# Gate and up products made transposed, with high and low tokens side by side in one 512-column product

## The reference

```
def swiglu_ffn(x, w_gu, w_down):
    a, u = jnp.split(x @ w_gu, 2, axis=-1)
    return (jax.nn.silu(a) * u) @ w_down

x = layer_norm(DEEPNORM_ALPHA * x + 0.5 * swiglu_ffn(x, ffn1_w_gu[l], ffn1_w_down[l]), ...)
```

## Time and profile before

| | |
|---|---|
| median of 3 runs | 1339.62 us (1339.14 to 1340.37) |
| span of the profiled execution | 1336.4 us |
| TensorE busy | 1316.4 us (99%) |
| VectorE busy | 1017.8 us (76%) |
| ScalarE busy | 677.8 us (51%) |
| mean DMA rate | 199 GB/s |
| chain that ended last | TensorE 85%, VectorE 7%, ScalarE 3%, DMA 2% |

### The profile page before, as it was taken

How to read it: one execution, slowest core, us unless ns; L and a number is a source line. 1 busy time by engine, 2 the same in 40 slices (tenths; PEclk the granted TensorE clock), 3 DMA queues, 4 the chain that set the end, 5 groups by cost and what they waited for, 6 DMA issues and landing times.

```text
span 1336.4 us, 18974 instructions
## 1 busy us (share of the span) xinstructions
PE 1316.4 (99%) x7172; PEld 1117.9 (84%) x7172; DVE 1017.8 (76%) x1597; ACT 677.8 (51%) x1069; POOL 105.0 (8%) x153
## 2 busy tenths in 40 slices
PE   9999999999999999999999999999999999999997
PEld 7888888788888888888887888888889998799985
DVE  6676778887777677777688887677776789966897
ACT  6444445644544445444437534444446668357582
POOL 1011000011011001111010010111000000000000
PEclk9999999999999999999999999999999999999999
DMA  8976756438766657676656449677556563465530
GB/s 270 321 237 227 228 181 213 129 102 262 239 233 226 199 189 243 228 235 218 210 171 207 126 137 322 236 249 235 173 192 175 157 206 127 142 194 163 183 127 32
DMA packets 199210, 265.46 MB, mean 199 GB/s; under 512 B 21392, under 2 KB 144400, under 8 KB 198608
## 3 DMA queue, kind: packets, MB, share of 16 engines
q1 hardware_dynamic: 187408, 223.65, 51.7%
q0 software_dynamic: 11712, 40.60, 8.9%
HBM read 263.13 MB, written 1.07 MB: 198 GB/s over the span
## 4 chain that ended last, share of the span: by engine, by line
PE 85%; DVE 7%; ACT 3%; DMA 2%; issue 1%; SPq 0%; DVEq 0%; ACTq 0%
PE ps L814 26%; PE ps L815 26%; PE ps L816 26%; PE ps L898 4%; DVE w_lo L1306 2%; DMA w_raw<-in_ffn_w_gu 1%; ACT w_hi L1134 1%; PE ps L1042 1%; PE ps L1103 1%; ACT att L1242 1%; DMA w_raw<-in_w_in 1%; DVE arena L1597 1%; DVE few_first L1335 1%; PE ps L1077 1%; DVE y L1334 1%
## 5 line engine op out<-in xcount | busy, mean ns | idle before, releaser
L1306 DVE TENSOR_TENSOR w_lo<-w_raw,w_hi 128x1024 fp32r<-128x1024 f32 (+3 forms) x424 | 499.1, 1206 | 143.4 <-ACT w_hi L1134 140.2
L1134 ACT ACTIVATE w_hi<-w_raw 128x1024 fp32r<-128x1024 f32 (+3 forms) x424 | 433.2, 1046 | 243.3 <-DMA w_raw<-in_ffn_w_gu 129.4
L814 PE MATMUL ps<-w_hi,col_hi 128*128 128x512 f32 (+2 forms) x1024 | 396.4, 387 | 3.6 <-DVE w_lo L1306 2.2
L816 PE MATMUL ps<-w_hi,col_lo 128*128 128x512 f32 (+2 forms) x1024 | 391.4, 382 | 0.0
L815 PE MATMUL ps<-w_lo,col_hi 128*128 128x512 f32 (+2 forms) x1024 | 391.2, 382 | 0.0
L814 PEld LDWEIGHTS ps<-w_hi,col_hi 128*128 128x128 f32 x1024 | 192.7, 188 | 42.7 <-DVE w_lo L1306 4.0
L816 PEld LDWEIGHTS ps<-w_hi,col_lo 128*128 128x128 f32 x1024 | 192.4, 188 | 37.2
L815 PEld LDWEIGHTS ps<-w_lo,col_hi 128*128 128x128 f32 x1024 | 192.8, 188 | 33.8
L814 PE MATMUL ps<-w_hi,lat_hi 128*128 128x512 f32 (+2 forms) x544 | 208.9, 384 | 0.0
L816 PE MATMUL ps<-w_hi,lat_lo 128*128 128x512 f32 (+2 forms) x544 | 206.6, 380 | 0.0
L815 PE MATMUL ps<-w_lo,lat_hi 128*128 128x512 f32 (+2 forms) x544 | 206.3, 379 | 0.0
(11 more groups left out here) (148 smaller groups left out, 1180.1 us busy)
## 6 DMA issues: line engine op xcount, KB each, us to landing
w_raw<-in_ffn_w_gu SPq DMA_DIRECT2D x352, 256.0 KB, 4.4
w_raw<-in_w_in SPq DMA_DIRECT2D x108, 512.0 KB, 4.6
w_raw<-in_ffn_w_down SPq DMA_DIRECT2D x88, 512.0 KB, 4.7
mod<-in_w_ada POOLq DMA_DIRECT2D x32, 768.0 KB, 7.3
w_raw<-in_w_out SPq DMA_DIRECT2D x24, 512.0 KB, 4.5
norm_g<-in_ln_g POOLq DMA_DIRECT2D x8, 512.0 KB, 4.1
norm_b<-in_ln_b POOLq DMA_DIRECT2D x8, 512.0 KB, 5.7
w_raw<-in_w_out SPq DMA_DIRECT2D x16, 256.0 KB, 4.4
```

The costliest lines, as they stand in the source:

```text
L814: pe.matmul(dst, a_hi, b_hi, start=start, stop=False)
L816: return pe.matmul(dst, a_lo, b_hi, start=False, stop=stop)
L1134: act.activation(half_of(w_hi[j], n, h), half_of(raw[j], n, h), ACT.Copy).then_inc(hi_ready, 1)
L1306: tt(half_of(w_lo[j], n, h), half_of(raw[j], n, h), half_of(w_hi[j], n, h).bitcast(F32), ALU.subtract)\
```

## The change

From round 2 on (`BY_ROWS = 2`) the gate and up products are made transposed. Job `gt(r, m, part)` makes 128 hidden columns (`m` = 0 or 1) of the gate (`part` 0) or of up (`part` 1) for all 256 tokens. The stationary operand is now a 128-column tile of the weights, the moving operand the transposed tokens. High and low tokens lie side by side in one tile `col`, so that one product of 512 columns gives high weight x (high tokens, low tokens) in one bank, and one of 256 columns adds low weight x high tokens to its left half. Sixteen such products, eight of each kind, make one group, and four groups make a round. Each group has a bank of its own among 4, 5 and 6 in turn (`gt_bank`).

VectorE adds the two halves of the bank by one TENSOR_REDUCE over pairs, the gate's into `silu_rows`, the up's into `hidden`. ScalarE takes silu in place in SBUF, and VectorE multiplies. The result already has hidden columns on the partitions, so the transposes of rounds 2 to 10 are gone. Job `hcol` (per `m`) makes high and low parts straight from SBUF. Rounds 0 and 1 stay as they were, with `ht` for both. The `ht` of round 1 now comes after the first group of round 2.

A weight unit of gate and up is used in all four groups of a round, half the group for each unit. Unit (r,1) is first needed after 8 products, and unit (r,0) is given back after seven eighths of the round's gate and up work, where it was three quarters.

```
 ROUNDS = F // FU
 TAIL = 4
+BY_ROWS = 2
...
     for r in range(2, ROUNDS):
-        jobs += gu(r, 0) + [("ht", s, r - 1)]
+        jobs += gt(r, 0, 0) + [("ht", s, r - 1) if r - 1 < BY_ROWS else ("hcol", s, r - 1, 1)] + gt(r, 0, 1)
         if r > 2:
             jobs += [("spread", s, r - 3), ("modrow", s, r - 3)]
         if r < 2 + MOD_STEPS:
             jobs += [("modsum", s, r - 2)]
-        jobs += gu(r, 1)
+        jobs += gt(r, 1, 0) + [("hcol", s, r, 0)] + gt(r, 1, 1)
...
-    jobs += down(tail[0], 0) + down(tail[1], 0) + [("ht", s, ROUNDS - 1)] + down(tail[2], 0) + down(tail[3], 0)
+    jobs += down(tail[0], 0) + down(tail[1], 0) + [("hcol", s, ROUNDS - 1, 1)] + down(tail[2], 0) + down(tail[3], 0)
...
+def gt_bank(r, m, part):
+    return 4 + (4 * (r - BY_ROWS) + 2 * m + part) % 3
...
-        col_hi, _ = sb("col_hi", [P, KT, S], F32R)
-        col_lo, _ = sb("col_lo", [P, KT, S], F32R)
+        col, _ = sb("col", [P, KT, 2, S], F32R)
+        col_hi, col_lo = col[:, :, 0, :], col[:, :, 1, :]
...
+                elif kind == "gt":
+                    r, m, part, h = job[2:]
+                    if h == 0:
+                        bank_ready((s, r, m, part))
+                        if (r, gt_bank(r, m, part)) == (BY_ROWS, 6):
+                            turns_done(("ht", s, BY_ROWS - 1))
+                    for i in range(TT):
+                        tile_ready(s, i, h)
+                    hi, lo = parts_of(n)
+                    cols = slice(part * FU + m * P, part * FU + (m + 1) * P)
+                    b = gt_bank(r, m, part)
+                    for k in range(4):
+                        if k == 2:
+                            unit_ready(n, j, 1)
+                        kk = 4 * h + k
+                        if kk < KT - 1:
+                            pe.matmul(bank(b), hi[:, k, cols], col[:, kk, :, :].rearrange("p a s -> p (a s)"), start=kk == 0, stop=False)
+                        last = pe.matmul(bank(b, S), lo[:, k, cols], col_hi[:, kk, :], start=False, stop=False)
+                        if kk == KT - 1:
+                            last = pe.matmul(bank(b), hi[:, k, cols], col[:, kk, :, :].rearrange("p a s -> p (a s)"), start=False, stop=True)
+                    signal_end(last, n, j, (s, r, m, part) if h == 1 else None)
...
                 elif kind == "down":
                     r, i = job[2:]
-                    turns_done(("ht", s, r))
+                    if r < BY_ROWS:
+                        turns_done(("ht", s, r))
+                    else:
+                        pe.wait_ge(h_cols, at["h_cols", (s, r, 1)])
...
+                elif kind == "gt":
+                    r, m, part, h = job[2:]
+                    nth = at["silu", job[1:4]]
+                    if (part, h) == (1, 0):
+                        act.wait_ge(summed, at["summed", (s, r, m, 0)])
+                        act.activation(silu_rows[:, nth % 2, :], silu_rows[:, nth % 2, :], ACT.Silu).then_inc(silu_done, 1)
+                elif kind == "hcol":
+                    r, m = job[2:]
+                    act.wait_ge(hidden_done, at["hidden", (s, r, m)])
+                    act.activation(lat_hi[:, 2 * (r % 4) + m, :], hidden[:, r % 2, m, :], ACT.Copy).then_inc(hi_part, 1)
...
+                elif kind == "gt" and job[5] == 1:
+                    r, m, part, _ = job[2:]
+                    nth = at["hidden", job[1:4]]
+                    rows = silu_rows[:, nth % 2, :] if part == 0 else hidden[:, r % 2, m, :]
+                    name, value = ENDS[job[1:5]]
+                    dve.wait_ge(ends[name], value)
...
+                    dve.tensor_reduce(rows, bank(gt_bank(r, m, part)).rearrange("p (a s) -> p s a", a=2), AX_X, ALU.add).then_inc(summed, 1)
+                    if part == 1:
+                        dve.wait_ge(summed, at["summed", job[1:5]])
+                        dve.wait_ge(silu_done, nth)
+                        stt(rows, silu_rows[:, nth % 2, :], 0.5, rows, ALU.mult, ALU.mult).then_inc(hidden_done, 1)
+                elif kind == "hcol":
+                    r, m = job[2:]
+                    dve.wait_ge(hi_part, at["hi_part", job])
+                    q = 2 * (r % 4) + m
+                    tt(lat_lo[:, q, :], hidden[:, r % 2, m, :], lat_hi[:, q, :].bitcast(F32), ALU.subtract).then_inc(h_cols, 1)
```

More of the change, by code:

```diff
@@ L167, in ffn_jobs @@
     down = lambda r, i: [("down", s, r, i)]
+    gt = lambda r, m, part: [("gt", s, r, m, part, h) for h in range(2)]
     if s == 0:
@@ L282, in unit_of @@
         return s, ("gu", job[2], job[4])
+    if kind == "gt":
+        return s, ("gu", job[2], job[5])
     if kind == "down":
@@ L306, in columns_of @@
     ks, width, _ = unit_shape(*unit_of(job))
+    if kind == "gt":
+        return ks * width // 2
     if kind == "row":
@@ L421, in count_jobs @@
             turns[b] += 1
-        if kind in ("gu", "row", "T") and s != stage:
+        if kind in ("gu", "gt", "row", "T") and s != stage:
             held, step, readers, stage, buffers = {}, None, {}, s, []
@@ L426, in count_jobs @@
             n = NUMBER[got]
[L427 to L432, removed]
+            if kind == "gt":
+                first_half, last_half = (job[5] == h for h in range(2))
+                tile, group = None, job[1:5]
+            else:
+                last_half = kind in ("T", "down", "out") or job[4] == (1 if kind == "gu" else len(BLOCKS[KIND[s]][job[2]][0]) - 1)
+                first_half = kind in ("T", "down", "out") or job[4] == 0
+                tile = None if kind == "T" else job[3]
+                group = (s, job[2], tile) if kind in ("gu", "row") else (s, got[1], tile)
+            if kind in ("gu", "gt", "row", "T"):
+                bank = {"gu": lambda: gu_bank(s, job[2], tile), "gt": lambda: gt_bank(*job[2:5]),
                         "row": lambda: BLOCKS[KIND[s]][job[2]][3][tile], "T": lambda: TURNED[got[1]][0]}[kind]()
@@ L440, in count_jobs @@
                         held[bank] = ("hidden", COUNT.value["hidden", group])
+                    elif kind == "gt":
+                        COUNT.add("summed", group)
+                        COUNT.add(("silu", "hidden")[job[4]], job[1:4])
+                        held[bank] = ("summed", COUNT.value["summed", group])
                     elif not (kind == "row" and job[2] == "KV" and tile == 0):
@@ L455, in count_jobs @@
                     ENDS["sums", s, tile] = ENDS[group]
-        if kind in ("xt", "ht", "trlat", "ycols"):
+        if kind in ("xt", "ht", "hcol", "trlat", "ycols"):
             COUNT.add("hi_part", job)
+        if kind == "hcol":
+            COUNT.add("h_cols", job[1:])
         if kind == "ycols" and not TURN[job]:
@@ L838, in bank_ready @@
                     name, value = BANK_BEFORE[group]
-                    pe.wait_ge({"hidden": hidden_done, "copied": copied}[name], value)
+                    pe.wait_ge({"hidden": hidden_done, "summed": summed, "copied": copied}[name], value)
             def signal_end(last, n, j, group):
```

9 lines of the change are left out of this document (7 added, 2 removed).

## The result

| | before | after |
|---|---|---|
| median of 4 runs, us | 1339.99 (1339.14 to 1341.33) | 1352.67 (1351.30 to 1356.43) |
| span of the profiled execution, us | 1336.4 | 1349.2 |
| TensorE busy, us | 1316.4 | 1316.7 |
| VectorE busy, us | 1017.8 | 1106.7 |

The ratio is 1.0099, 95% interval 1.0086 to 1.0112. The change costs 1.0%. The forecast was 1341.4 in a range of 1334 to 1350, so the time lies above the range.

What follows compares the result with a forecast made beforehand. TensorE, busy 99% of the span, was taken as the bound. Its own -4.9 us plus stalls of 0.5, 2.9, 1.1, 0.4, 1.1 and 0.7 gave +1.8: span 1338.2, median 3.2 above it, so 1341.4 us, range 1334 to 1350.

Steps and rivals of the forecast that it cites:

- Ordinary rounds lose little: First sum done just in time for the fourth group in ordinary rounds; 0.5 us lost for all of them.
- T: The start of a round on TensorE; the fourth group was reckoned to start 8.6 us after it.
- Lateness shrinking: VectorE's round from first sum to next takes 15.4 us, under TensorE's 16.88, so lateness shrinks 1.5 us a round.
- TensorE's own work: Rounds from round 2 on: transposes give back 0.35 us, products add 0.21; 16.88 instead of 17.02, -4.9 us in all.
- The sum's price: Each VectorE sum of a bank's halves takes 0.686 us; VectorE's net added work is 2.9 us a round.
- The rival of a strided sum at 1.22 us: Reading PSUM with a step slows each sum, making VectorE the bound: about 1361 us; chance 0.10.
- the one of a pair at 0.36: Rival: a 512 and a 256 column product on TensorE together cost 0.36 us: about 1356 us; chance 0.05.
- The first bank in ordinary rounds: Fourth group wants the first group's bank 8.6 us into the round; its sum is done at 7.1 to 8.5.
- The rival with a stall in every round: Slipping loads make 28 modulated rounds wait at the first bank, 0.3 to 0.5 us each: about 1350; chance 0.20.
- Stage 0, round 3: TensorE waits 1.5 us for splits of unit (3,1) and 1.35 for the modulation's low part, together 2.9 us.
- Stages 3 and 5, round 2: Round 1's "ht" comes late and the third group needs its bank: 0.4 us lost in stage 3, 1.1 in stage 5.
- The 1 MB load and the fold: Stage 5: a load in flight delays the split, 1.1 us lost; the fold's 3.5 us on VectorE, 0.7 lost.

Runs made afterwards that it cites:

- e2: Kernel after the change with down products of three rounds instead of four left for the end, so round 9 has them too: 1352.74 us, ratio 1.0100.
- e3: Kernel after the change with round 9's 3.5 us modulation sum on VectorE moved behind the third group's sum: 1345.50 us, ratio 1.0045.
- e5: Kernel after the change without the four sums of a round, result missing high weights times low tokens: 1336.54 us, ratio 0.9980.
- e1: Kernel after the change with products grouped by length (four of 512 columns, eight of 256, four of 512) instead of in turn: 1347.05 us, ratio 1.0059.
- after_again: Kernel after the change, unchanged, run a second time beside the kernel before: 1351.31 us, ratio 1.0106.
- e4: Kernel after the change with each TENSOR_REDUCE replaced by a ScalarE copy to SBUF and a two-input VectorE add: 1348.36 us, ratio 1.0068.

## Why the prediction was wrong

Against its own sum, -4.9 + 6.7 = +1.8 us of span, the span grew by 12.8.

- **What failed: one bank's deadline stood for all of them, and ordinary rounds for all rounds.** The prediction asks when the first group's bank is wanted ("The fourth group of a round overwrites the first group's bank, so it needs the first sum") and lets lateness shrink from there. It never asks when the third group's bank is wanted, and by its sum "Ordinary rounds lose little" covers rounds 9 and 10 as well. In rounds 3 to 8 the third sum is in time by 3 us or more. In round 9 TensorE has no down products, and it wants that bank 5.4 us earlier, at T + 14.3, while VectorE ends the sum 8.85 us after the start of the first one. The list of places that lose doesn't have the last rounds, and they cost 8.1 us of the 12.8. e2, with down products in round 9, and e3, with the chain behind the third sum, each take those waits away, and in e5, without sums, nothing is lost there.
- **It could have been reckoned**: the order of the jobs leaves out `down` in the last two rounds, before shows the distance of 11.56 us, and with the prediction's own first sum, done at T + 7.1 to 8.5, the third, which by the traces of after ends 8.2 us behind it, would be done at T + 15.3 to 16.7, 1.0 to 2.4 us late in each of four stages. The busy time alone wouldn't have shown it: 7.66 of 11.56 us before, and 2.9 more.
- **Lateness shrinking**: 15.4 us were reckoned from a first sum to the next one. In stage 0, where VectorE has no pause from round 3 to round 4, it is 15.1; in round 9 it is 10.4 under TensorE's 11.5. So this step held.
- **TensorE's own work**: -4.9 was reckoned, 36 x -0.07 = -2.5 measured. The pair is 0.3525 us, 0.0058 above the sum of the two spacings (+0.19 a round), and the modulation pair 0.20 instead of 0.29, which wasn't foreseen (-0.09). By e1 about half of the first comes from changing the length in turn (0.10 a round). The direction was right; the gain was mis-sized by 2.4 us. The Trainium skill, "TensorE: Matmul & The Clock Gate", section "Back-to-back issue gap", would put a pair at 0.325 us by its formula for an isolated product; the trace shows 0.3525, and the measurement decides.
- **The sum's price**: 0.686 forecast, 0.683 measured. VectorE's added busy time is 88.9 us, 2.5 a round; 2.9 was reckoned. The rival of a strided sum at 1.22 us is refuted. So is the one of a pair at 0.36, whose 1356 us is in any case the forecast plus 15 and not, as it says, the floor plus 15.
- **The first bank in ordinary rounds**: the first sums of stage 2 start between T + 5.15 and T + 6.95 in rounds 3 to 8 and end by T + 7.6; they are wanted at T + 8.6, so no loss, within the forecast's 0.5 us. In rounds 4 to 8 of all stages the latest end is T + 8.4, but for the round behind the fold, where it is T + 8.8. The rival with a stall in every round came nearest to the time (1350) by a mechanism that didn't happen; that nearness is luck.
- **Stage 0, round 3**: 1.5 and 1.35 us were forecast, for the splits of (3,1) and for the modulation's low part. The timeline of after:

```profile
50.09 0.39 PE L970 MATMUL ps<-col,w_hi 128*128 128x512 f32 x1
...
53.24 0.50 PE L970 MATMUL ps<-col,w_hi 128*128 128x512 f32 x1 [1.59 <-DVE w_lo L1360]
...
54.38 0.50 PE L970 MATMUL ps<-col,w_hi 128*128 128x512 f32 x1 [0.17 <-DVE w_lo L1360]
...
59.04 0.36 PE L983 MATMUL ps<-ada_hi,ones 128*128 128x192 f32 x1 [0.91 <-DVE ada_lo L1485]
```

  1.59 + 0.17 and 0.91, at the places forecast. With the slow first product after each wait the stretch from 50.09 to 59.04 is 8.95 us where 5.64 is TensorE's work: 3.3 lost, 2.9 forecast. The mechanism held; that the size fits so well is partly luck, since with the same order there the first wait is 0.86 us in after_again, 0.66 in e2 and 0.62 in e3, and 2.3 to 2.6 us are lost.
- **Stages 3 and 5, round 2**: the later stages' starts lost 2.7 us together, 1.5 were forecast. In stage 5 the waits are for splits (0.33 and 0.35 near 827), not for the "ht" as reckoned, and in stage 2, where none was forecast, 0.85 at the transposes of x, which after_again doesn't have.
- **The 1 MB load and the fold** (stage 5, rounds 5 and 7): 1.1 and 0.7 forecast; the distances of after show 0 and 0.29. Other kernels with sums lose between 0.05 (e1) and 1.5 (e4) at the fold, 0.55 in e3 and 1.2 in e2, and in the load's round only e1 does, 1.1. So both sizes occur, but not in each execution; 0.7 was fair for the fold, and 1.1 for the load was the bad case taken for the usual one.

What stays open: why loads land as late as they do in round 9 of stages 0 and 2 after the change. Before, the last split ahead of the sum's place started in stage 2 at T + 3.6; after, it starts at T + 7.0, and no run here moves the loads by themselves. The waits of round 9 and 10 take their size from that. Open too is why lengths in turn cost more than lengths in groups.

## What to carry to other kernels

"The engine has room in a round" isn't enough, even where it is true: take each result that the bottleneck engine waits for, and compare when it is wanted with when it is done. Do so for each kind of round, above all the first and the last ones, where the bottleneck engine has less to do in between. Work with a close deadline (a sum that frees a bank) should stand ahead of long work without one (a 3.5 us chain), and moving that one chain was worth 5 to 7 us here, more than the whole gain that the change was able to bring. Making the bottleneck's end longer doesn't mend it if that end was the cover of something else (e2).

## What the runs showed of the hardware

- A TENSOR_REDUCE on VectorE from PSUM over pairs 256 values apart takes 683 ns for 512 values, as much as a two-input operation of 512; an add of 256 with one input in PSUM 420 ns.
- Alternating products of 512 and 256 columns start 0.3525 us apart per pair, grouped by eight 0.3475; three of 256 columns take 0.36.
- The product behind TensorE's first one after a wait starts late: 53.24 to 53.58, 0.34 us, and 464.38 to 464.71, 0.33 us, where 0.235 is usual.
